# Two transformer blocks on one core: the last down product's second token tile in three pieces, and a last store of 256 columns

## The chip, the cores and the metric

One NeuronCore of a Trainium2 chip runs the whole program in one launch. The metric is the device time of that launch in microseconds. Three runs of the kernel before took 749.52, 749.52 and 749.61 us; their median is 749.52 us.

## The reference

The input is one sequence of 256 tokens by 1024 channels (float32). A first block (three mixers, then a gated feed-forward) and a second block (spatial gating, block-sparse attention, convolution, cross attention, then a feed-forward of 4096 hidden channels) follow each other. The change touches only the end of the second block, its last two lines:

```python
        h = rms_norm(x, pre_ffn_g[l])
        f = jnp.square(jax.nn.relu(h @ w_ff1[l])) @ w_ff2[l]
        x = x + rms_norm(f, post_ffn_g[l])
    return x
```

`rms_norm(f, g)` divides each token's 1024 values by the root of their mean square (plus 1e-6) and multiplies by `g`. So no element of the output can be formed before the last of the token's 1024 sums of `h @ w_ff2` is complete.

## The kernel before, in words

Tokens lie in two tiles of 128 (`t` = 0, 1), one token to a partition; `P` = 128, `T` = 256, `NB` = 512, `TT` = 2. Each float32 weight is split into a high part (ACT, a rounding copy) and a low part (DVE, L1318, raw minus high), and so is each activation; `mm3` (L2076 to L2080) makes one product from three matmuls: low activations by high weights, high by low, high by high. The program is written as one instruction stream for each engine (PE, ACT, DVE, POOL, and SP, which issues most DMAs), with semaphores between them. Each engine works through its stream in the written order.

The second feed-forward runs in 8 chunks of 512 hidden channels. The down product adds over all chunks into four banks of PSUM, each 128 partitions by 512 float32: banks 4 and 5 hold the left and right half (columns 0 to 511, 512 to 1023) of token tile 0, banks 6 and 7 those of token tile 1. The last chunk is done by `last_down` (L2155): token tile 0 first, both halves together (24 matmuls of 512 columns: 4 k-tiles, 2 halves, 3 matmuls), then token tile 1's left half (12 matmuls into bank 6), then its right half (12 into bank 7). PE raises `tile0_used` after tile 0 and after the left half, and `w_used` after each weight group of the right half.

What follows is `post_acc`, written once for ACT (L1093) and once for DVE (L1801). For each token tile, in the order tile 0, tile 1:

- ACT squares each half from its bank and adds up each row into `sums` (the Square with `accum_out`, traced as an ACTIVATE and an ACTIVATION_READ_ACCUMULATOR), and raises `post_sum`.
- DVE multiplies each half by the feed-forward's scale `inv` and the gain `row_g` into `xn` (L1809, "the gain" below), and raises `zg`; between the halves it adds 1e-6 to the first half's sum (L1812).
- ACT takes the root of both sums together (Sqrt with the other sum as bias) and raises `post_sd`.
- DVE takes the reciprocal (L1815), then adds `xn` times it to `x`, half by half (L1819, "the final sums"), and raises `x_ready` for each.

The same semaphore `zg` counts the gains of an earlier `post_norm` too: 8 of them before `post_acc` begins. SP waits for each `x_ready` in turn and issues four stores of 128 tokens by 512 columns (256 KB, rows of 2 KB; L562), then waits until all four have landed (L563), and that ends the program. ACT and DVE each finish tile 0's part of `post_acc` before they take up tile 1's, in the written order.

Of the kernel before, what the change touches and what calls it, by code (L numbers as in the profile page):

```python
# [14 lines left out]
P = 128  # L15
T = 256
# [242 lines left out]
def two_blocks(nc, w, out):  # L259
# [3 lines left out]
    with ctx:  # L263
        def sb(name, shape, dt=F32):
            return ctx.enter_context(nc.sbuf_tensor(name, shape, dt))
# [32 lines left out]
        inv = sb("inv", [P, 2 * TT])  # L298
        half_rstd = sb("half_rstd", [P, TT])
        sums = sb("sums", [P, TT, 2])  # L300
        var = sb("var", [P, 32])
        rstd = sb("rstd", [P, 32])
        tiny = sb("tiny", [P, 40])
# [187 lines left out]
        NORM_GAIN = ["norm_mix_g", "norm_ffn_g", "pre_mix_g_2", "mem_g_2", "pre_x_g_2", "pre_ffn_g_2"]  # L491
        X_READY_END = 4 + 4 + 2 + 5 * TT
        FINAL, POST = 6, 7
        SQRT_2_PI = math.sqrt(2 / math.pi)
        block = ctx.enter_context(nc.Block())

# [29 lines left out]
        def _(sp):  # L526
# [29 lines left out]
                                 src[row:row + n * P, c:c + cw].rearrange("(k p) n -> p k n", p=P))\  # L556
                      .then_inc(raw_in[g % RAW], 16)

            for t in range(TT):
                for c in range(2):  # L560
                    sp.wait_ge(sem.x_ready, X_READY_END - 2 * TT + 1 + 2 * t + c)
                    sp.dma_start(out[t * P:(t + 1) * P, c * NB:(c + 1) * NB], x[:, t, c * NB:(c + 1) * NB])\  # L562
                      .then_inc(sem.stored, 16)  # L563
            sp.wait_ge(sem.stored, 32 * TT)

        @block.gpsimd
        def _(pool):
# [150 lines left out]
        def _(act):  # L718
# [3 lines left out]
            def f(dst, src, func, **k):  # L722
                return act.activation(dst, src, func, **k)  # L723
# [369 lines left out]
            def post_acc():  # L1093
                for t in range(TT):
                    act.wait_ge(sem.ffn_scale, t + 1)
                    for c in range(2):
                        if c == 0:
                            act.wait_ge(sem.tile0_used, me.seen("tile0_used"))
                        elif t == 1:
                            act.wait_ge(sem.w_used, me.used)  # L1100
                        f(post_junk[:, t, c * NB:(c + 1) * NB], bank[4 + 2 * t + c][:, :], ACT.Square,
                          scale=inv[:, TT + t:TT + t + 1], accum_out=sums[:, t, c:c + 1]).then_inc(sem.post_sum, 1)
                    k = 2 * (POST + 2) + t
                    act.wait_ge(sem.post_sum, 8 + 2 * t + 2)
                    act.wait_ge(sem.left_sum, t + 1)
                    f(rstd[:, k:k + 1], sums[:, t, 1:2], ACT.Sqrt, bias=var[:, k:k + 1]).then_inc(sem.post_sd, 1)

            def x_exp(i):

# [192 lines left out]
        def _(dve):  # L1302
# [498 lines left out]
            def post_acc():  # L1801
                for t in range(TT):
                    k = 2 * (POST + 2) + t
                    for c in range(2):
                        dve.wait_ge(sem.post_sum, me.seen("post_sum"))
                        if c == 0 and t == 0:
                            dve.wait_ge(sem.row_in, me.seen("row_in", 16))
                        cut = slice(c * NB, (c + 1) * NB)
                        stt(xn[:, t, cut], bank[4 + 2 * t + c][:, :], inv[:, t:t + 1], row_g[:, cut], MUL, MUL)\  # L1809
                            .then_inc(sem.zg, 1)  # L1810
                        if c == 0:
                            ts(var[:, k:k + 1], sums[:, t, 0:1], EPS, None, ADD).then_inc(sem.left_sum, 1)  # L1812
                    dve.wait_ge(sem.zg, me.seen("zg", 2))
                    dve.wait_ge(sem.post_sd, t + 1)
                    dve.reciprocal(rstd[:, k:k + 1], rstd[:, k:k + 1]).then_inc(sem.dve_step, 1)  # L1815
                    dve.wait_ge(sem.dve_step, me.step())
                    for c in range(2):
                        cut = slice(c * NB, (c + 1) * NB)
                        stt(x[:, t, cut], xn[:, t, cut], rstd[:, k:k + 1], x[:, t, cut], MUL, ADD)\  # L1819
                            .then_inc(sem.x_ready, 1)  # L1820

            def kv_low(c, pair):
# [247 lines left out]
        def _(pe):  # L2070
# [85 lines left out]
            def last_down(c):  # L2156

                parts = chunks[("down2", c)]
                for t in range(TT):
                    for ns in ((0, 1),) if t == 0 else ((0,), (1,)):  # L2160
                        for g, kts in parts:
                            pe.wait_ge(low_sem(g), before(g))
                            wh, wl = part(high, g), part(low, g)
                            for j, kt in enumerate(kts):
                                in_h, in_l = (half[:, kt, t * P:(t + 1) * P] for half in hidden_of(c, False))
                                for n in ns:
                                    cut = slice(n * NB, (n + 1) * NB)
                                    ins = mm3(bank[4 + 2 * t + n][:, :], in_h, in_l, wh[:, j, cut], wl[:, j, cut],
                                              False, kt == 3)
                            if t == 1 and ns == (1,):  # L2170
                                ins.then_inc(sem.w_used, 1)
                        if t == 0 or ns == (0,):
                            ins.then_inc(sem.tile0_used, 1)

            def branch_products(i, mid=None):
# [509 lines left out]
```

## Time and profile before

| what | value |
|---|---|
| median of three runs | 749.52 us (749.52 to 749.61) |
| the profiled execution's own time | 749.77 us |
| its span (first to last event on the core) | 748.0 us |
| PE busy, share of the span | 740.5 us, 99% |
| DVE busy | 523.8 us, 70% |
| ACT busy | 402.5 us, 54% |
| POOL busy | 49.7 us, 7% |
| granted TensorE clock, mean | 1.0 of full speed |

The profile comes from one execution, whose own time is 0.25 us above the median and 1.77 us above its span. Times in the views are counted from the span's start, in microseconds, durations of groups in nanoseconds. PE is the matmul stream, PEld the loading of weights into it, DVE the vector engine, ACT the scalar engine, SPq the queue of SP's DMA issues. A matmul's end is modelled, its start is recorded. "idle" in a row is the engine's time without work just before, and what ended it.

### The profile page before, as it was taken

To read this page: it belongs to the slowest core of one execution; us is meant where nothing else is said; L and a number is where in the kernel's file an instruction comes from. 1 tells how busy PE (TensorE), PEld (TensorE's weight loads), DVE (VectorE), ACT (ScalarE), POOL (GpSimd) and SP (SyncE) were. 2 spreads that over 40 slices of the span, in tenths; PEclk is the share of its full clock that TensorE was granted. 3 is DMA by queue.
4 is the path that set the end of the run, shared out by engine and by line. 5 is a ranking of instruction groups with operands and counts; after the bars stand their busy time and mean duration, and the time that the engine had idled before them with its cause. 6 is when DMAs were issued, how large, how long until landed. Compare 5 with 4: busy or idle time off the path is not lost.

```text
span 748.0 us, 10384 instructions
## 1 busy us (share of the span) xinstructions
PE 740.5 (99%) x4280; PEld 648.8 (87%) x4280; DVE 523.8 (70%) x612; ACT 402.5 (54%) x509; POOL 49.7 (7%) x71
## 2 busy tenths in 40 slices
PE   9999999999999999999999999999999999999996
PEld 9988888889988888888899898789988988888885
DVE  6788946885766666656779998785758655556564
ACT  6678378544545545444653685673647443454442
POOL 0200002120000000000230200030003000000000
PEclk9999999999999999999999999999999999999999
DMA  9866365555565556666466536365065466555431
GB/s 337 280 224 225 137 237 210 171 171 168 176 219 169 170 171 204 215 203 209 154 218 205 165 117 225 116 235 165 21 212 166 162 221 225 172 199 188 162 123 57
DMA packets 74239, 138.42 MB, mean 185 GB/s; under 512 B 3916, under 2 KB 28368, under 8 KB 74064
## 3 DMA queue, kind: packets, MB, share of 16 engines
q1 hardware_dynamic: 72336, 132.69, 52.9%
q10 hardware_dynamic: 1856, 5.06, 1.9%
q8 instruction: 34, 0.56, 0.3%
q14 instruction: 13, 0.11, 0.0%
HBM read 136.69 MB, written 1.05 MB: 184 GB/s over the span
## 4 chain that ended last, share of the span: by engine, by line
PE 97%; DVE 2%; issue 0%; ACT 0%; DVEq 0%; ACTq 0%
PE wide L2074 70%; PE bank L2074 25%; PE bank L2198 2%; DVE low L1318 0%; DVE arena L1581 0%; ACT arena L723 0%; DVE act_hl L1415 0%; DVE xn L1809 0%; DVE x L1819 0%; DVE arena L1641 0%; DVE arena L1637 0%; DVE hid_l L1646 0%; DVE arena L1643 0%; DVE arena L1627 0%; DVEq L263 0%
## 5 line engine op out<-in xcount | busy, mean ns | idle before, releaser
L1318 DVE TENSOR_TENSOR low<-raw,high 128x2048 fp32r<-128x2048 f32 (+1 forms) x118 | 267.0, 2279 | 106.2 <-ACT high L723 101.5
L723 ACT ACTIVATE high<-raw 128x2048 fp32r<-128x2048 f32 (+3 forms) x134 | 234.7, 1770 | 122.8 <-PE wide L2074 95.9
L2074 PE MATMUL wide<-act_hl,high 128*128 128x256 f32 (+1 forms) x1184 | 241.3, 327 | 0.0
L2074 PEld LDWEIGHTS wide<-act_hl,high 128*128 128x128 f32 x1184 | 198.9, 191 | 18.3 <-issue 0.2
L2074 PE MATMUL wide<-high,act_hl 128*128 128x512 f32 x528 | 170.1, 394 | 0.5 <-DVE arena L1581 0.2
L2074 PE MATMUL wide<-act_hl,low 128*128 128x256 f32 x832 | 161.2, 284 | 0.0
L2074 PEld LDWEIGHTS wide<-act_hl,low 128*128 128x128 f32 x832 | 128.6, 192 | 2.8 <-DVE low L1366 0.2
L2074 PEld LDWEIGHTS wide<-high,act_hl 128*128 128x128 f32 x528 | 99.1, 188 | 23.3 <-issue 1.7
L2074 PE MATMUL wide<-low,act_hl 128*128 128x512 f32 x264 | 103.0, 390 | 0.0
L2074 PE MATMUL bank<-high,hid_l 128*128 128x512 f32 x216 | 84.4, 391 | 0.3 <-DVE hid_l L1646 0.3
L2074 PE MATMUL bank<-low,hid_h 128*128 128x512 f32 x216 | 84.2, 390 | 0.0
L2074 PE MATMUL bank<-high,hid_h 128*128 128x512 f32 x216 | 84.0, 389 | 0.0
L723 ACT ACTIVATE arena<-wide 128x512 f32<-128x512 f32 x53 | 29.5, 596 | 86.3 <-PE wide L2074 86.3
L2074 PEld LDWEIGHTS wide<-low,act_hl 128*128 128x128 f32 x264 | 49.7, 188 | 9.3
L2074 PEld LDWEIGHTS bank<-high,hid_l 128*128 128x128 f32 x216 | 40.6, 188 | 8.6 <-DVE hid_l L1646 0.7
L2074 PEld LDWEIGHTS bank<-high,hid_h 128*128 128x128 f32 x216 | 40.6, 188 | 8.6
L2074 PEld LDWEIGHTS bank<-low,hid_h 128*128 128x128 f32 x216 | 40.6, 188 | 7.8
L1627 DVE TENSOR_TENSOR arena<-wide,arena 128x512 f32<-128x512 f32 x30 | 20.7, 689 | 28.7 <-ACT arena L723 28.5
L1442 DVE SCALAR_TENSOR_TENSOR arena<-arena,vec 128x256 f32<-128x256 f32 x78 | 38.3, 536 | 0.9
L723 ACT ACTIVATE hid_h<-arena 128x512 fp32r<-128x512 f32 x27 | 16.8, 635 | 29.0 <-DVE arena L1643 16.9
L723 ACT ACTIVATE arena<-arena 128x512 f32<-128x512 f32 (+5 forms) x31 | 19.5, 651 | 21.4 <-DVE arena L1637 14.5
L588 POOL TENSOR_SCALAR var<-sums 128x1 f32<-128x1 f32 x8 | 6.0, 748 | 316.1 <-ACT xn L723 208.5
(215 smaller groups left out, 681.1 us busy)
## 6 DMA issues: line engine op xcount, KB each, us to landing
raw<-in_w_ff_dram SPq DMA_DIRECT2D x32, 1024.0 KB, 5.3
raw<-in_w_in_dram SPq DMA_DIRECT2D x27, 1024.0 KB, 5.3
raw<-in_w_ffn_in_dram SPq DMA_DIRECT2D x44, 512.0 KB, 4.9
raw<-in_w_ffn_out_dram SPq DMA_DIRECT2D x11, 1024.0 KB, 6.5
raw<-in_w_xkv_dram SPq DMA_DIRECT2D x8, 1024.0 KB, 5.0
raw<-in_w_o_dram SPq DMA_DIRECT2D x4, 1024.0 KB, 5.1
raw<-in_w_out_dram SPq DMA_DIRECT2D x4, 1024.0 KB, 5.0
raw<-in_w_xq_dram SPq DMA_DIRECT2D x4, 1024.0 KB, 5.2
```

Of the source, the lines that this page charges most:

```text
L588: pool.tensor_scalar(v, sums[:, t, 0:1], sums[:, t, 1:2], EPS, ALU.add, ALU.add)\
L723: return act.activation(dst, src, func, **k)
L1318: tt(part(low, g), part(raw, g), f32(part(high, g)), SUB).then_inc(sem.low_by_dve, 1)
L1442: ins = stt(tile_of(dst, c), window, weight(j, c), tile_of(dst, c), MUL, ADD)
L1627: tt(in2(h_low[b]), wide_of(b, 0), in2(h_low[b]), ADD).then_inc(sem.hid_sum, 1)
L2074: return pe.matmul(dst, lhs, rhs, start=start, stop=stop, skip_group_check=loose)
L2198: return pe.transpose(dst, src, ident[0:n, 0:n])
```

## The change

`last_down` does token tile 1 in three pieces, named by `LAST_SPANS`: columns 512 to 767 (the third quarter, in the first half of bank 7), columns 0 to 511 (the left half, bank 6), and columns 768 to 1023 (the fourth quarter, in the second half of bank 7). Before the third piece PE waits until `zg` is 11 (`FIRST_OUT`): 8 earlier gains, 2 of tile 0, and tile 1's first one, of the third quarter. `post_acc` handles tile 1 in the same three pieces on both engines, with a third sum `third_sum`; DVE adds the first two sums and 1e-6 after the second gain. The final sums of tile 1 are of 256, 512 and 256 columns. The stores of tile 1 are three: the third quarter's is issued from ACT's queue, those of the left half and the fourth quarter from SP's. `stored` is waited for to 80 instead of 64 (five stores).

```diff
+        third_sum = sb("third_sum", [P, 1])
...
+        LAST_SPANS = (NB, T), (0, NB), (NB + T, T)
+        FIRST_OUT = 2 * 2 * TT + 2 + 1
+        last_sums = (sums[:, 0, 0:1], sums[:, 0, 1:2]), (sums[:, 1, 0:1], sums[:, 1, 1:2], third_sum[:, :])
...
-            for t in range(TT):
-                for c in range(2):
-                    sp.wait_ge(sem.x_ready, X_READY_END - 2 * TT + 1 + 2 * t + c)
-                    sp.dma_start(out[t * P:(t + 1) * P, c * NB:(c + 1) * NB], x[:, t, c * NB:(c + 1) * NB])\
-                      .then_inc(sem.stored, 16)
-            sp.wait_ge(sem.stored, 32 * TT)
+            for i, (t, a, size) in enumerate(((0, 0, NB), (0, NB, NB), (1, 0, NB), (1, NB + T, T))):
+                sp.wait_ge(sem.x_ready, X_READY_END - 2 * TT + (1, 2, 4, 5)[i])
+                sp.dma_start(out[t * P:(t + 1) * P, a:a + size], x[:, t, a:a + size]).then_inc(sem.stored, 16)
+            sp.wait_ge(sem.stored, 80)
...
             def post_acc():
                 for t in range(TT):
                     act.wait_ge(sem.ffn_scale, t + 1)
-                    for c in range(2):
-                        if c == 0:
+                    for i, (a, size) in enumerate(LAST_SPANS if t else ((0, NB), (NB, NB))):
+                        if i < 2 and i <= t:
                             act.wait_ge(sem.tile0_used, me.seen("tile0_used"))
                         elif t == 1:
                             act.wait_ge(sem.w_used, me.used)
-                        f(post_junk[:, t, c * NB:(c + 1) * NB], bank[4 + 2 * t + c][:, :], ACT.Square,
-                          scale=inv[:, TT + t:TT + t + 1], accum_out=sums[:, t, c:c + 1]).then_inc(sem.post_sum, 1)
+                        f(post_junk[:, t, a:a + size], bank[4 + 2 * t + a // NB][:, a % NB:a % NB + size], ACT.Square,
+                          scale=inv[:, TT + t:TT + t + 1], accum_out=last_sums[t][i]).then_inc(sem.post_sum, 1)
                     k = 2 * (POST + 2) + t
-                    act.wait_ge(sem.post_sum, 8 + 2 * t + 2)
+                    act.wait_ge(sem.post_sum, 8 + (2, 5)[t])
                     act.wait_ge(sem.left_sum, t + 1)
-                    f(rstd[:, k:k + 1], sums[:, t, 1:2], ACT.Sqrt, bias=var[:, k:k + 1]).then_inc(sem.post_sd, 1)
+                    f(rstd[:, k:k + 1], last_sums[t][-1], ACT.Sqrt, bias=var[:, k:k + 1]).then_inc(sem.post_sd, 1)
+                act.wait_ge(sem.x_ready, X_READY_END - 1)
+                act.dma_start(out[P:2 * P, NB:NB + T], x[:, 1, NB:NB + T]).then_inc(sem.stored, 16)
...
-                    for c in range(2):
+                    spans = LAST_SPANS if t else ((0, NB), (NB, NB))
+                    for i, (a, size) in enumerate(spans):
                         dve.wait_ge(sem.post_sum, me.seen("post_sum"))
...
+                        stt(xn[:, t, a:a + size], bank[4 + 2 * t + a // NB][:, a % NB:a % NB + size], inv[:, t:t + 1],
+                            row_g[:, a:a + size], MUL, MUL).then_inc(sem.zg, 1)
+                        if t == 0 and i == 0:
                             ts(var[:, k:k + 1], sums[:, t, 0:1], EPS, None, ADD).then_inc(sem.left_sum, 1)
+                        elif t == 1 and i == 1:
+                            ts(var[:, k:k + 1], sums[:, t, 0:1], sums[:, t, 1:2], EPS, ADD, ADD).then_inc(sem.left_sum, 1)
...
-                    for ns in ((0, 1),) if t == 0 else ((0,), (1,)):
+                    for piece in range(1 if t == 0 else 3):
+                        spans = LAST_SPANS[piece:piece + 1] if t else ((0, NB), (NB, NB))
+                        if piece == 2:
+                            pe.wait_ge(sem.zg, FIRST_OUT)
                         for g, kts in parts:
...
-                            if t == 1 and ns == (1,):
+                            if t == 1 and piece == 2:
                                 ins.then_inc(sem.w_used, 1)
-                        if t == 0 or ns == (0,):
+                        if t == 0 or piece < 2:
                             ins.then_inc(sem.tile0_used, 1)
```

PE's stream at the border between the last two pieces of token tile 1. Before, from the left half (bank 6) to the right half (bank 7):

```order
L2074 MATMUL bank6<-high0,hid_l1 128x512
L2074 MATMUL bank6<-low0,hid_h1 128x512
L2074 MATMUL bank6<-high0,hid_h1 128x512
L2074 MATMUL bank7<-high2,hid_l1 128x512 [waits low_by_dve]
L2074 MATMUL bank7<-low2,hid_h1 128x512
L2074 MATMUL bank7<-high2,hid_h1 128x512
```

and in the change, from the left half to the fourth quarter:

```order
L2079 MATMUL bank6<-high0,hid_l1 128x512
L2079 MATMUL bank6<-low0,hid_h1 128x512
L2079 MATMUL bank6<-high0,hid_h1 128x512
L2079 MATMUL bank7<-high2,hid_l1 128x256 [waits low_by_dve,zg]
L2079 MATMUL bank7<-low2,hid_h1 128x256
L2079 MATMUL bank7<-high2,hid_h1 128x256
```

The last piece has 12 matmuls of 256 columns instead of 12 of 512, and its first one waits for `zg`; 12 more of 256 columns into bank 7 now stand ahead of the left half's.

DVE's stream from tile 0's final sums on. Before:

```order
L1819 SCALAR_TENSOR_TENSOR x<-xn,rstd,x 128x512 [waits dve_step]
L1819 SCALAR_TENSOR_TENSOR x<-xn,rstd,x 128x512
L1809 SCALAR_TENSOR_TENSOR xn<-bank6,inv,row_g 128x512 [waits post_sum]
L1812 TENSOR_SCALAR var<-sums 128x1
L1809 SCALAR_TENSOR_TENSOR xn<-bank7,inv,row_g 128x512 [waits post_sum]
L1815 RECIPROCAL rstd<-rstd 128x1 [waits post_sd,zg]
L1819 SCALAR_TENSOR_TENSOR x<-xn,rstd,x 128x512 [waits dve_step]
L1819 SCALAR_TENSOR_TENSOR x<-xn,rstd,x 128x512
```

and in the change:

```order
L1824 SCALAR_TENSOR_TENSOR x<-xn,rstd,x 128x512 [waits dve_step]
L1824 SCALAR_TENSOR_TENSOR x<-xn,rstd,x 128x512
L1813 SCALAR_TENSOR_TENSOR xn<-bank7,inv,row_g 128x256 [waits post_sum]
L1813 SCALAR_TENSOR_TENSOR xn<-bank6,inv,row_g 128x512 [waits post_sum]
L1818 TENSOR_SCALAR var<-sums 128x1
L1813 SCALAR_TENSOR_TENSOR xn<-bank7,inv,row_g 128x256 [waits post_sum]
L1821 RECIPROCAL rstd<-rstd 128x1 [waits post_sd,zg]
L1824 SCALAR_TENSOR_TENSOR x<-xn,rstd,x 128x256 [waits dve_step]
L1824 SCALAR_TENSOR_TENSOR x<-xn,rstd,x 128x512
L1824 SCALAR_TENSOR_TENSOR x<-xn,rstd,x 128x256
```

The third quarter's gain, whose `zg` PE waits for, stands right behind tile 0's two final sums, and the small addition of the sums has moved behind the second gain.

## Rows read from the trace of the kernel before

**Rows 1.** the page, part 4: the chain that ended last, shares of the span

```profile
PE 97%; DVE 2%; issue 0%; ACT 0%; DVEq 0%; ACTq 0%
```

**Rows 2.** timeline (start us, us, engine, line, operation, tiles): ACT and DVE to the end

```profile
740.18 0.67 ACT L723 ACTIVATE arena<-bank,inv 128x512 f32<-128x512 f32 x1
...
740.57 1.42 DVE L1819 SCALAR_TENSOR_TENSOR x<-xn,rstd,x 128x512 f32<-128x512 f32 x2
...
741.90 0.74 DVE L1809 SCALAR_TENSOR_TENSOR xn<-bank,inv,row_g 128x512 f32<-128x512 f32 x1
...
742.36 0.69 ACT L723 ACTIVATE arena<-bank,inv 128x512 f32<-128x512 f32 x1 [1.42 <-PE bank L2074]
...
742.94 0.19 ACT L723 ACTIVATION_READ_ACCUMULATOR arena<-bank,inv 128x1 f32 x1
...
743.17 0.75 DVE L1809 SCALAR_TENSOR_TENSOR xn<-bank,inv,row_g 128x512 f32<-128x512 f32 x1 [0.47 <-ACT arena L723]
743.96 0.16 DVE L1815 RECIPROCAL rstd<-rstd 128x1 f32<-128x1 f32 x1
744.15 1.42 DVE L1819 SCALAR_TENSOR_TENSOR x<-xn,rstd,x 128x512 f32<-128x512 f32 x2
```

**Rows 3.** SP's queue in the timeline: the last store's issue

```profile
745.59 0.33 SPq L562 DMA_DIRECT2D out_dram<-x  x1
```

**Rows 4.** the output stores' line: time to landing

```profile
DMA to landing us min/median/max: 2.0/2.0/2.1
```

**Rows 5.** timeline of PE: token tile 1's first and last matmul

```profile
736.72 0.39 PE L2074 MATMUL bank<-high,hid_l 128*128 128x512 f32 x1
...
741.93 0.39 PE L2074 MATMUL bank<-high,hid_h 128*128 128x512 f32 x1
```

**Rows 6.** timeline of PE: sixteen matmuls of 256 columns in a row

```profile
718.46 2.08 PE L2074 MATMUL wide<-act_hl,low 128*128 128x256 f32 x16
```

**Rows 7.** instructions grouped by line and shape, DVE: xcount, busy us, mean ns, idle

```profile
L1442 DVE SCALAR_TENSOR_TENSOR arena<-arena,vec 128x256 f32<-128x256 f32 x78 | 38.3, 536 | 0.9
...
L1383 DVE SCALAR_TENSOR_TENSOR act_hl<-bank,vec,act_hl 128x256 fp32r<-128x256 f32 x24 | 9.8, 477 | 2.9 <-ACT act_hl L723 2.9
...
L1809 DVE SCALAR_TENSOR_TENSOR xn<-bank,inv,row_g 128x512 f32<-128x512 f32 x4 | 3.0, 747 | 7.3 <-ACT arena L723 7.3
...
L1512 DVE SCALAR_TENSOR_TENSOR arena<-arena 128x256 f32<-128x256 f32 x2 | 0.8, 425 | 0.1
```

**Rows 8.** timeline: PE held by DVE and started again, an earlier down product

```profile
357.61 0.69 DVE L1646 TENSOR_TENSOR hid_l<-arena,hid_h 128x512 fp32r<-128x512 f32 x1 [0.70 <-ACT hid_h L723]
...
358.35 0.50 PE L2074 MATMUL bank<-high,hid_l 128*128 128x512 f32 x1 [0.26 <-DVE hid_l L1646]
...
358.69 0.40 PE L2074 MATMUL bank<-low,hid_h 128*128 128x512 f32 x1
```

**Rows 9.** instructions grouped by line and shape, ACT

```profile
L723 ACT ACTIVATE arena<-wide,half_rstd 128x512 f32<-128x512 f32 x12 | 7.6, 685 | 11.0 <-PE wide L2074 11.0
...
L723 ACT ACTIVATE arena<-bank,neg_max,rstd 128x256 f32<-128x256 f32 x8 | 4.5, 560 | 8.1 <-DVE neg_max L1856 8.0
...
L723 ACT ACTIVATE arena<-wide,half_rstd 128x256 f32<-128x256 f32 x2 | 0.9, 450 | 0.0
```

**Rows 10.** timeline of DVE: eight operations of 256 columns in a row

```profile
133.31 3.25 DVE L1383 SCALAR_TENSOR_TENSOR hid_l<-xn,vec,hid_h 128x256 fp32r<-128x256 f32 x8
```

**Rows 11.** stretches: us, PE, PEld, DVE, ACT, POOL busy (x), PEclk, DMA share, GB/s

```profile
745.00:746.00 1.00, 0.00 (x0) 0.00 (x0) 0.57 (x1) 0.00 (x0) 0.00 (x0) 1.00 0.22 84
746.00:747.00 1.00, 0.00 (x0) 0.00 (x0) 0.00 (x0) 0.00 (x0) 0.00 (x0) 1.00 1.04 385
...
747.40:748.00 0.60, 0.00 (x0) 0.00 (x0) 0.00 (x0) 0.00 (x0) 0.00 (x0) 0.53 0.00 0
```

**Rows 12.** DMA issues of loads: xcount, KB each, median us to landing

```profile
raw<-in_w_ff_dram SPq DMA_DIRECT2D x32, 1024.0 KB, 5.3
...
raw<-in_w_ffn_in_dram SPq DMA_DIRECT2D x44, 512.0 KB, 4.9
```

More of the change, by code:

```diff
@@ L1803, in post_acc @@
                     k = 2 * (POST + 2) + t
-                    for c in range(2):
+                    spans = LAST_SPANS if t else ((0, NB), (NB, NB))
+                    for i, (a, size) in enumerate(spans):
                         dve.wait_ge(sem.post_sum, me.seen("post_sum"))
-                        if c == 0 and t == 0:
+                        if i == 0 and t == 0:
                             dve.wait_ge(sem.row_in, me.seen("row_in", 16))
[L1808 to L1811, printed above, removed]
+                        stt(xn[:, t, a:a + size], bank[4 + 2 * t + a // NB][:, a % NB:a % NB + size], inv[:, t:t + 1],
+                            row_g[:, a:a + size], MUL, MUL).then_inc(sem.zg, 1)
+                        if t == 0 and i == 0:
                             ts(var[:, k:k + 1], sums[:, t, 0:1], EPS, None, ADD).then_inc(sem.left_sum, 1)
-                    dve.wait_ge(sem.zg, me.seen("zg", 2))
+                        elif t == 1 and i == 1:
+                            ts(var[:, k:k + 1], sums[:, t, 0:1], sums[:, t, 1:2], EPS, ADD, ADD).then_inc(sem.left_sum, 1)
+                    dve.wait_ge(sem.zg, me.seen("zg", len(spans)))
                     dve.wait_ge(sem.post_sd, t + 1)
@@ L1816, in post_acc @@
                     dve.wait_ge(sem.dve_step, me.step())
-                    for c in range(2):
-                        cut = slice(c * NB, (c + 1) * NB)
-                        stt(x[:, t, cut], xn[:, t, cut], rstd[:, k:k + 1], x[:, t, cut], MUL, ADD)\
+                    for a, size in spans:
+                        stt(x[:, t, a:a + size], xn[:, t, a:a + size], rstd[:, k:k + 1], x[:, t, a:a + size], MUL, ADD)\
                             .then_inc(sem.x_ready, 1)
@@ L2165, in last_down @@
                                 in_h, in_l = (half[:, kt, t * P:(t + 1) * P] for half in hidden_of(c, False))
[L2166 to L2169, printed above, removed]
-                            if t == 1 and ns == (1,):
+                                for a, size in spans:
+                                    cut = slice(a, a + size)
+                                    ins = mm3(bank[4 + 2 * t + a // NB][:, a % NB:a % NB + size], in_h, in_l,
+                                              wh[:, j, cut], wl[:, j, cut], False, kt == 3)
+                            if t == 1 and piece == 2:
                                 ins.then_inc(sem.w_used, 1)
-                        if t == 0 or ns == (0,):
+                        if t == 0 or piece < 2:
                             ins.then_inc(sem.tile0_used, 1)
```

## The prediction

> **What bounds the kernel now.** I read the page's chain first: 97% of the span is PE's work [rows 1], so until the last down product nothing but PE's own pace counts, and the change leaves all of that alone. What is left is the end, and for it I read the timeline of the last engines [rows 2] and SP's queue [rows 3]. PE's last matmul starts at 741.93 and ends, as modelled, at 741.93 + 0.39 = 742.32 [rows 5]. Then one thing follows another: the Square of the right half (742.36), its accumulator read (742.94), the right half's gain on DVE (743.17), the reciprocal (743.96), two final sums (744.15 to 745.57) [rows 2], the last store's issue at 745.59 [rows 3] and its landing 2.0 us later [rows 4], at 747.59. The span ends 0.4 us after that. The reader is to see two things: the tail from PE's end to the landing is 5.27 us, in which halving the last piece can save something; and DVE is not idle before it. Tile 0's final sums run from 740.57 to 741.99, and only then, at 741.90 (the rows overlap by 0.08), does DVE take the left half's gain, although ACT had squared that half from 740.18 on [rows 2]. DVE is late with tile 0 when tile 1 comes.
>
> **PE's pieces.** Twelve matmuls of 512 columns become 24 of 256. 512 columns come every (741.93 - 736.72) / 23 = 0.227 us [rows 5]; sixteen of 256 take 2.08 us, the last one 0.28, so one every 0.12 us [rows 6]. Without any wait, the third quarter would run from 736.72 to 738.16, the left half to 740.88, and the fourth quarter's last matmul would start at 742.20 and end at 742.48: 0.16 later than before.
>
> **The new wait.** The fourth quarter's first matmul waits for the third quarter's gain. ACT can have squared that quarter by about 740.8: it starts at 740.18 as it now starts the left half [rows 2], and the piece is smaller. But on DVE the gain stands behind tile 0's two final sums, which nothing in the change moves. It takes the place that the left half's gain has now, 741.90 [rows 2]. A gain of 256 columns isn't in the trace. The nearest row is DVE's operation of the same kind, from a bank with a per-token scalar, 477 ns (bounds: 425 without the scalar, 536 for the slowest of 256 columns; 512 columns take 747) [rows 7]. So `zg` reaches 11 at 741.90 + 0.48 = 742.38. An earlier down product shows what a restart costs: DVE's operation ended at 357.61 + 0.69 = 358.30, PE started at 358.35, and the second matmul came 0.34 after the first instead of 0.23 [rows 8]. So PE starts at 742.43, its twelfth matmul at 742.43 + 0.11 + 11 x 0.12 = 743.86, and it ends at 744.14. PE stands for 742.43 - 740.88 = 1.55 us, and ends **1.82 us later** than before. Behind the waiting instruction on PE is only this piece, and ACT's last Square waits for it. The left half's gain meanwhile runs on DVE from 742.30 to 743.05, and the addition of the sums behind it, both under PE's last piece: nothing. If that cover went, they would add 0.75 + 0.14.
>
> **The tail behind it.** The Square of 256 columns: a pair of rows gives 685 ns for 512 columns and 450 for 256 of the same operation, so 0.24 less (bound: an accumulating one of 256 took 560, only 0.12 less) [rows 9]. The gain: 0.75 to 0.48, 0.27 less; the Sqrt beside it (0.29) is still shorter. The reciprocal stays. The final sums: two of 512 columns took 1.42. Now there are three. Eight operations of 256 columns took 3.25 us, the last one 0.48, so one every 0.40 [rows 10]; 512 ones come 1.42 - 0.75 = 0.67 apart. 0.40 + 0.67 + 0.48 = 1.55, 0.13 more. Sum on DVE: +1.82 - 0.24 - 0.27 + 0.13 = +1.44, so its last sum ends at 747.01, and its first begins at 747.01 - 1.55 = 745.46.
>
> A rule speaks against the change here. The Trainium skill, page "VectorE: DVE Perf Modes", section on the TRN2 errata, says that operations pay a fixed part each and should be of 512 elements or more. Its estimate for float32, (N + 151) / 0.96 ns, gives 424 ns for 256 columns and 691 for 512; by it the gain that PE waits for is 0.05 shorter, the last gain saves 0.27 as above, and three sums cost 0.16 us more than two, so the sum would be +1.42. The trace agrees with the slope (270 ns for 256 columns, 747 less 477) if not with the level.
>
> **The stores.** Before, the two stores of tile 1 moved 524 KB: 84 KB up to 746, 385 KB in the next microsecond, the rest after it [rows 11]. At 385 GB/s they were done at 747.14, 0.45 before the landing, and a 256 KB store takes 0.68, so its data begins 2.0 - 0.45 - 0.68 = 0.87 after the issue. Now the third quarter's store is issued by ACT near 745.97 and is through by 747.2. The left half's sum ends at 745.46 + 0.40 + 0.75 = 746.61, its store is issued at 746.63, its data begins at 747.50. The fourth quarter's is issued at 747.03, so its data would begin at 747.90, but the left half's occupy the engines until 748.18. 393 KB from 747.50 take 1.02: 748.52, landing at 748.97, **+1.38**. If landing were 2.0 whatever the size, it would be 749.03, +1.44. Whether rows of 1 KB move as fast as rows of 2 KB: weight loads of two times 512 KB (1 KB rows) land after 4.9 us, of 1024 KB (2 KB rows) after 5.3 [rows 12]; the second half is issued some 0.4 later, so yes. Two queues in place of one, and the fifth store's semaphore, I cost at nothing: the third quarter's store has over 1 us of cover.
>
> **Sum:** +1.4 us. Bounds: no restart cost, and gains at 425: -0.11 - 0.05 - 0.05 - 0.05, so +1.1. Gains at 536, the Square at 560, the last store at the full 0.68: +0.06 for each of three operations, +0.11, +0.34, so +2.0. The profiled execution would take 749.77 + 1.4 = 751.2; it stands 0.25 above the median, so against the median of 749.52 I forecast **750.9 us**. That is 0.19%, and 0.2% (1.5 us) is about what a measurement of this kernel can tell from no change: the forecast lies just inside it.
>
> **Rivals.**
> 1. *The last store costs a whole one* (slower, beyond 0.2%). If 128 rows of 1 KB occupy the DMA engines as long as 128 rows of 2 KB, the last landing moves by 0.34: +1.7, 751.2 us. It decides from 0.1 us above my sum on. For it: the store waits behind the left half's. Against it: rows 12. I count with it the case that small operations stand near their upper bounds. 27%.
> 2. *The clock falls in the gap.* At 1.2 instead of 2.4 GHz the twelve matmuls would take 1.3 us more: +2.7, 752.2 us. Against it: after PE's end the granted clock was still 1.00 at 746 to 747, over 4 us later, and only then 0.53 [rows 11]; the gap is 1.55 us. 3%.
> 3. *PE isn't held.* If `zg` passes before 740.9, because the count or DVE's order is another than the text says, PE ends at 742.48: +0.16 - 0.24 - 0.27 + 0.13 - 0.06 = -0.3 us, 749.2 us. That is what the change would give if DVE were free in time. Against it: the 8 earlier gains and tile 0's two leave 11 to tile 1's first, and DVE's order is fixed. 4%, of which 1% for more than 0.2% faster.
>
> **The numbers.** The forecast has 66%, 11 of them above +1.5. Slower by over 0.2%: 11 + 27 + 3 = 41%; faster 1%; within 0.2%, the rest: 58%. The range takes the bounds +1.1 to +2.0 and goes a little beyond them, to 750.4 and 751.6; it leaves out rivals 2 and 3 and the far tails.
>
> **What would show it.** PE idle from about 740.9 to 742.4, released by DVE's gain, twelve matmuls of 256 columns behind it at clock 1.00, PE's end near 744.1; Square about 0.45, gains about 0.48, three final sums in 1.55; last store issued near 747.0, span near 749.4. The argument is wrong if PE shows no gap, if the gap ends at another time than DVE's first small gain, or if the last landing comes over 2.1 us after its issue.

## The result

| | before | the change |
|---|---|---|
| median, 14 runs each | 749.56 us (749.06 to 750.07) | 751.02 us (750.58 to 751.36) |
| ratio to before, 95% interval | | 1.0019 [1.0012, 1.0026] |
| span of the profiled execution | 748.0 us | 749.3 us |
| granted TensorE clock, mean | 1.0 | 0.999 |

The kernel became slower by 1.46 us; the forecast was 1.4 us, 750.9, in a range of 750.4 to 751.6. By the 0.2% that the text had set, it lies just within "no change", yet the interval excludes 1: with 14 runs a side it is 0.07% wide to each side, finer than that bound. Of the runs below, one of twelve of the kernel "third quarter early" (4046.16 us) and one of eleven of that kernel with halves and the early table (2616.61 us) took several times as long, at a mean granted clock of 1.0 and for a reason that no trace shows; the medians include them (without them 749.40 in place of 749.44 and 749.18 in place of 749.19), the ratios do not.

The page of the kernel after: its first line, and the busy times.

```profile
span 749.3 us, 10414 instructions
...
PE 740.7 (99%) x4292; PEld 649.5 (87%) x4292; DVE 523.9 (70%) x614; ACT 402.8 (54%) x511; POOL 49.7 (7%) x71
```

PE has twelve more matmuls and 0.2 us more work; nothing there explains 1.5 us. The end of the timeline does (start us, us, engine, line, operation, tiles, count, in brackets the idle time before it and what ended it). The rows answer to [rows 2] and [rows 5].

```profile
740.32 0.19 ACT L725 ACTIVATION_READ_ACCUMULATOR arena<-bank,inv 128x1 f32 x1
740.36 1.41 DVE L1824 SCALAR_TENSOR_TENSOR x<-xn,rstd,x 128x512 f32<-128x512 f32 x2
740.46 0.39 PE L2079 MATMUL bank<-high,hid_h 128*128 128x512 f32 x1
...
741.69 1.14 DVE L1813 SCALAR_TENSOR_TENSOR xn<-bank,inv,row_g 128x256 f32<-128x256 f32 x2
...
742.22 0.39 PE L2079 MATMUL bank<-high,hid_l 128*128 128x256 f32 x1 [1.37 <-DVE xn L1813]
...
742.44 0.28 PE L2079 MATMUL bank<-low,hid_h 128*128 128x256 f32 x1
...
743.64 0.28 PE L2079 MATMUL bank<-high,hid_h 128*128 128x256 f32 x1
743.95 0.47 ACT L725 ACTIVATE arena<-bank,inv 128x256 f32<-128x256 f32 x1 [2.29 <-PE bank L2079]
744.33 0.19 ACT L725 ACTIVATION_READ_ACCUMULATOR arena<-bank,inv 128x1 f32 x1
...
744.55 0.48 DVE L1813 SCALAR_TENSOR_TENSOR xn<-bank,inv,row_g 128x256 f32<-128x256 f32 x1 [1.61 <-ACT arena L725]
745.07 0.16 DVE L1821 RECIPROCAL rstd<-rstd 128x1 f32<-128x1 f32 x1
745.27 1.54 DVE L1824 SCALAR_TENSOR_TENSOR x<-xn,rstd,x 128x256 f32<-128x256 f32 x3
```

In this execution everything up to token tile 1 came 0.22 us earlier than in that of before: tile 1's first matmul starts at 736.50, before at 736.72 [rows 5]. Below, times are therefore compared from that first matmul on, called T0. The reader is to see: ACT has read the third quarter's sum by 740.51 (740.32 + 0.19), but DVE is busy until 741.77 with tile 0's two final sums and takes the third quarter's gain at 741.69, the first of the two operations in that row. The left half's last matmul starts at 740.46, so PE was ready for the fourth quarter at 740.69; its next matmul starts at 742.22. That is T0 + 5.72, where the forecast had T0 + 5.71. The list of waits names the releaser (who waited, for whom; us in all, times, longest):

```profile
PE bank L2079 <- DVE xn L1813: 1.4, 1, 1.4
```

The 1.37 us are counted from the modelled end of the matmul before; from the moment at which PE could have gone on it is 1.53.

The granted clock stays whole over the gap and behind it (columns as in [rows 11]):

```profile
741.00:742.00 1.00, 0.00 (x0) 0.00 (x0) 1.00 (x3) 0.66 (x2) 0.00 (x0) 1.00 0.02 8
742.00:743.00 1.00, 0.78 (x6) 0.79 (x7) 0.94 (x3) 0.00 (x0) 0.00 (x0) 1.00 1.00 373
743.00:744.00 1.00, 0.92 (x8) 0.71 (x6) 0.00 (x0) 0.05 (x1) 0.00 (x0) 1.00 0.38 143
```

The last store's issue on SP's queue, the third quarter's on ACT's, and the landings (issues: count, KB each, median us to landing):

```profile
746.84 0.48 SPq L565 DMA_DIRECT2D out_dram<-x  x1
```

```profile
745.79 0.35 ACTq L1110 DMA_DIRECT2D out_dram<-x  x1
```

```profile
out_dram<-x SPq DMA_DIRECT2D x3, 256.0 KB, 2.1
out_dram<-x ACTq DMA_DIRECT2D x1, 128.0 KB, 1.8
out_dram<-x SPq DMA_DIRECT2D x1, 128.0 KB, 2.1
```

The last store of 128 KB is issued at 746.84 and lands 2.1 us later, no sooner than a store of 256 KB [rows 4]; alone, the third quarter's lands after 1.8.

### The profile page after: what moved, and what is told of

Read it like the earlier page. It is cut to its first block, busy times and chain, and to the rows that moved or that the text cites. A ratio compares the mean times of both kernels' runs of the same rounds, so it can differ in the third digit from the quotient of the medians.

```text
span 749.3 us, 10414 instructions
## 1 busy us (share of the span) xinstructions
PE 740.7 (99%) x4292; PEld 649.5 (87%) x4292; DVE 523.9 (70%) x614; ACT 402.8 (54%) x511; POOL 49.7 (7%) x71
## 3 DMA queue, kind: packets, MB, share of 16 engines
q10 hardware_dynamic: 2000, 5.19, 1.9%
## 4 chain that ended last, share of the span: by engine, by line
PE 93%; DVE 2%; DMA 2%; issue 1%; ACT 1%; SPq 0%; POOL 0%; DVEq 0%; ACTq 0%; POOLq 0%
PE wide L2079 67%; PE bank L2079 24%; PE bank L2206 2%; DMA x<-in_x_dram 1%; DMA raw<-in_w_in_dram 1%; DVE low L1322 0%; DVE x L1824 0%; ACT arena L725 0%; DVE arena L1585 0%; DVE xn L1813 0%; DVE act_hl L1419 0%; DVE low L1370 0%; POOL rstd L596 0%; ACT act_hl L725 0%; DVE hid_l L1650 0%
## 5 line engine op out<-in xcount | busy, mean ns | idle before, releaser
L2079 PE MATMUL bank<-high,hid_l 128*128 128x512 f32 (+1 forms) x220 | 85.2, 387 | 1.6 <-DVE xn L1813 1.4
L2079 PE MATMUL bank<-low,hid_h 128*128 128x512 f32 (+1 forms) x220 | 85.0, 386 | 0.0
L2079 PE MATMUL bank<-high,hid_h 128*128 128x512 f32 (+1 forms) x220 | 84.7, 385 | 0.0
```

Of the source, the lines that this page charges most:

```text
L2079: return pe.matmul(dst, lhs, rhs, start=start, stop=stop, skip_group_check=loose)
```

## The experiments

All medians below are of timed runs beside runs of the kernel before on the same chip. There are three such series, in which the kernel before took 749.53, 749.60 and 749.62 us (749.56 beside the change), so times of different series compare only to about 0.1 us. In a trace, "ready" is the start of the left half's last matmul plus 0.23 us, and PE's gap is the fourth quarter's first matmul less ready. The texts that were written ahead of the runs partly count it from the modelled end of the matmul before, which makes it 0.16 us shorter (1.37 for 1.53, 2.17 for 2.33).

### The third quarter early

```diff
 ACT:
+                    if t == 0:
+                        act.wait_ge(sem.ffn_scale, 2)
+                        act.wait_ge(sem.tile0_used, me.seen("tile0_used"))
+                        square(1, 0, *LAST_SPANS[0])
                     k = 2 * (POST + 2) + t
 DVE:
+                    if t == 0:
+                        gain(1, *LAST_SPANS[0])
                     dve.wait_ge(sem.zg, ...)
                     dve.wait_ge(sem.post_sd, t + 1)
                     dve.reciprocal(...)
```

(Shortened: `square` and `gain` are the change's own operations, put into helpers, and tile 1's own loops leave out the third quarter, which is already done.)

> Edit: on ACT the Square of the third quarter, and on DVE its gain, go ahead of token tile 0's root and reciprocal; all else is as in the change. Theory A (the change pays for PE's wait behind DVE's two final sums of tile 0, one for one): the gain ends near 739.5, before PE is ready for the fourth quarter (740.7 in the change's trace), so PE has no gap, neither the 1.53 us of standing nor the 0.11 us of restart; 751.0 - 1.6 = 749.4 us, span near 747.7. Theory B (the 1.5 us lie in the smaller operations and the fifth store): they are all still there, so the time stays within 0.4 us of 751.0.

Measured: 749.44 us, before 749.53, ratio 0.9998 [0.9989, 1.0007]. The timeline of DVE and PE:

```profile
738.01 1.13 DVE L1817 SCALAR_TENSOR_TENSOR xn<-bank,inv,row_g 128x512 f32<-128x512 f32 x2
...
740.30 1.42 DVE L1841 SCALAR_TENSOR_TENSOR x<-xn,rstd,x 128x512 f32<-128x512 f32 x2
740.31 0.28 PE L2096 MATMUL bank<-high,hid_l 128*128 128x256 f32 x1
...
741.63 0.28 PE L2096 MATMUL bank<-high,hid_h 128*128 128x256 f32 x1
```

The gain is the second of the two operations at 738.01 and over at 739.14, in time in which DVE used to wait for the root. PE's fourth quarter starts at 740.31 without a gap and ends at 741.91. The 1.6 us are gone, while the small operations and the fifth store are all still there. Theory B falls.

### The third quarter between tile 0's final sums

```diff
                     for i, (a, size) in enumerate(spans):
+                        if t == 0 and i == 1:
+                            gain(1, *LAST_SPANS[0])
                         stt(x[:, t, a:a + size], ...)
```

> Edit: on DVE alone, the gain of the third quarter goes between tile 0's two final sums instead of behind both. Theory A: zg reaches 11 one final sum (0.67 us) earlier, PE restarts near 741.55 on the change's clock instead of 742.22, and the time falls by 0.67 to 750.3 us. Theory B: no effect, 751.0 us.

Measured: 750.47 us, ratio 1.0011 [1.0003, 1.002]. One operation moved by one place on one engine:

```profile
740.94 0.48 DVE L1808 SCALAR_TENSOR_TENSOR xn<-bank,inv,row_g 128x256 f32<-128x256 f32 x1
...
741.33 0.74 DVE L1832 SCALAR_TENSOR_TENSOR x<-xn,rstd,x 128x512 f32<-128x512 f32 x1
...
741.47 0.39 PE L2087 MATMUL bank<-high,hid_l 128*128 128x256 f32 x1 [0.79 <-DVE xn L1808]
```

PE starts 0.05 us behind the end of the gain (741.42). Its gap is 0.95 us (the left half's last matmul starts at 740.29), 0.58 less than the change's, and the time 0.55 less.

### The root's table early

```diff
             def post_acc():
+                f(loaded[:, :], ones[:, 0:1], ACT.Sqrt)
                 for t in range(TT):
                     act.wait_ge(sem.ffn_scale, t + 1)
```

> Edit: one Sqrt of a single column on ACT ahead of the last part, while ACT is idle, so that the table for the root is loaded there and not between tile 0's Squares and its root (1.28 us). DVE's order stays as in the change. Theory A, one step further back (DVE is late with tile 0 because of the table load): tile 0's root is taken near 738.45, its final sums run from 739.3 to 740.7, the third quarter's gain ends near 741.1, PE's gap shrinks from 1.53 to about 0.5, the time falls by 1.0 to 750.0 us. Theory B, or a table load that is not what delays DVE: 751.0 us.

Measured: 749.87 us, ratio 1.0006 [0.9997, 1.0014]. In the change, ACT loads the table between tile 0's Squares and its root:

```profile
738.47 1.28 ACT L725 ACT_TABLE_LOAD   x1 [0.25 <-DVE var L1816]
```

and here that load is gone from this place:

```profile
738.20 0.29 ACT L725 ACTIVATE rstd<-sums,var 128x1 f32<-128x1 f32 x1 [0.27 <-DVE var L1817]
...
739.00 1.42 DVE L1825 SCALAR_TENSOR_TENSOR x<-xn,rstd,x 128x512 f32<-128x512 f32 x2
...
740.33 0.48 DVE L1814 SCALAR_TENSOR_TENSOR xn<-bank,inv,row_g 128x256 f32<-128x256 f32 x1
...
740.87 0.19 PEld L2080 LDWEIGHTS bank<-high,hid_l 128*128 128x128 f32 x1 [0.72 <-DVE xn L1814]
```

Tile 0's root is taken at 738.20, and DVE's final sums begin at 739.00, 2.77 us after T0 (736.23) instead of 3.86. The gain stands where it stood in the order, and PE's gap is 0.46 us (the left half's last matmul starts at 740.18). So the reason that DVE is late with tile 0 is shown too: the table load of 1.28 us between tile 0's Squares and its root.

### The early third quarter with halves at the end

```diff
-                    for a, size in spans:
+                    for a, size in ((0, NB), (NB, NB)):
                         stt(x[:, t, a:a + size], ...)
 SP: four stores of 512 columns as before; ACT's store goes; stored is waited for to 64
```

> Edit: as in the first of these kernels (third quarter early on ACT and DVE), but tile 1's final sums are two of 512 columns and its stores two of 256 KB from SP, as before the change. Theory A with the terms of the sum: two sums take 0.13 us less than three, and the last store of 256 KB, with no store to wait behind, lands 2.0 us after its issue; so 0.0 to 0.1 us faster than the first kernel, 749.3 us. Theory C (the last store of 256 columns is worth having): the first kernel is faster than this one by 0.2 to 0.3 us, the half transfer of 0.34 less the 0.13.

Measured: 749.08 us, before 749.53, ratio 0.9993 [0.9985, 1.0002]; faster than the first of these kernels by 0.36 us at the medians and by 0.21 in T0 to the span's end (10.96 against 11.17). Two final sums take

```profile
743.47 1.41 DVE L1839 SCALAR_TENSOR_TENSOR x<-xn,rstd,x 128x512 f32<-128x512 f32 x2
```

against 1.54 for three. Theory C falls: a last store of 256 columns brings nothing here. In the two traces three pieces of sums and five stores cost 0.21 us, more than the expected 0.0 to 0.1: 0.13 up to DVE's last sum (T0 + 8.67 against T0 + 8.54) and 0.08 behind it. How much more than that the 0.36 of the medians holds stays open, since the kernel "the order of the last sums" below has three sums and five stores too and came out 0.39 under its own kernel before, almost as far as this one (0.45).

### Both, and the early table in the kernel before

```diff
 the kernel "early third quarter with halves", and on ACT
             def post_acc():
+                f(loaded[:, :], ones[:, 0:1], ACT.Sqrt)
```

> Edit: the kernel with the third quarter early and tile 1's final sums and stores in halves, and in addition the root's table loaded early (one Sqrt of a single column before the last part). Theory A: PE no longer waits for DVE in either, so an earlier tile 0 has little left to give; DVE's left gain and the addition of the sums (742.29 to 742.71 in the first kernel's trace) end just at the last gain's start, and going early frees at most 0.05 us: 749.0 to 749.1 us, level with the kernel without it (749.08). Rival: DVE's lateness with tile 0 costs the end on its own, apart from PE's wait; then it is faster by 0.3 or more.

Measured: 749.19 us, before 749.60, ratio 0.9991 [0.9982, 1.0001]; T0 to the span's end 10.96 us, the same as without the early table.

```diff
 the kernel before, and on ACT
             def post_acc():
+                f(loaded[:, :], ones[:, 0:1], ACT.Sqrt)
```

> Edit: the kernel before, with the root's table loaded early and nothing else. Theory A: in the kernel before, DVE's lateness with tile 0 is hidden, since its left gain (to 742.6) is over before the right half's sum is read (743.13), so nothing changes: 749.5 us. Rival, as for the kernel above: the time falls by 0.3 or more, and part of what the early table gained in the change was not PE's wait.

Measured: 749.55 us, before 749.60, ratio 1.0002 [0.9992, 1.0011]; T0 to the span's end 11.30 us (747.8 less 736.50), against 11.28 in the kernel before. Together these two say that DVE's lateness with tile 0 costs nothing by itself: it is hidden in the kernel before and in the kernel with the third quarter early. Only the change's wait made it visible. So the 1.15 us that the early table brought to the change are put down to PE's wait, which was 1.07 us shorter.

### The third quarter's gain one place later

```diff
-        FIRST_OUT = 2 * 2 * TT + 2 + 1
+        FIRST_OUT = 2 * 2 * TT + 2 + 2
...
-                    for i, (a, size) in enumerate(spans):
+                    order = [(0, *spans[0]), (1, *spans[1])] if t == 0 else [(1, *spans[1]), (0, *spans[0]), (2, *spans[2])]
+                    for i, a, size in order:
```

(Shortened: DVE's waits for the sums follow the new order; ahead of the left half's gain it waits for two sums.)

> Edit: in the change, DVE does the left half's gain first and the third quarter's behind it, so that PE waits for the twelfth gain in place of the eleventh. Nothing else moves. Theory A: zg arrives one operation of 512 columns (0.67 us) later, PE's gap grows from 1.53 to 2.2 us and the time by 0.67 to 751.7 us. Theory B (the gap is mostly cover for something else): less than 0.3 us more.

Measured: 752.52 us (751.43 to 752.87, 5 runs), ratio 1.0036 [1.0023, 1.0049]. Neither theory had this: one run of five took 751.4, the other four 752.4 to 752.9, 0.8 us more than the wait accounts for.

```profile
742.26 0.47 DVE L1814 SCALAR_TENSOR_TENSOR xn<-bank,inv,row_g 128x256 f32<-128x256 f32 x1
742.78 0.29 PEld L2080 LDWEIGHTS bank<-high,hid_l 128*128 128x128 f32 x1 [2.59 <-DVE xn L1814]
...
743.16 0.42 PE L2080 MATMUL bank<-low,hid_h 128*128 128x256 f32 x1
...
745.30 0.41 PE L2080 MATMUL bank<-high,hid_h 128*128 128x256 f32 x1
```

The gap is 2.32 us, as meant (742.78 less 740.46). But the matmuls of 256 columns behind it come 0.21 us apart instead of 0.12. The stretches tell why (PEclk is the third figure from the end):

```profile
740.60:742.60 2.00, 0.02 (x1) 0.00 (x0) 2.00 (x5) 0.78 (x2) 0.00 (x0) 1.00 0.43 158
742.60:742.90 0.30, 0.12 (x1) 0.12 (x1) 0.13 (x1) 0.00 (x0) 0.00 (x0) 0.83 1.04 396
742.90:743.40 0.50, 0.50 (x3) 0.50 (x4) 0.00 (x0) 0.00 (x0) 0.00 (x0) 0.50 0.48 180
743.40:745.70 2.30, 2.30 (x11) 2.02 (x10) 0.00 (x0) 0.00 (x0) 0.00 (x0) 0.50 0.00 0
```

The granted clock is 1.00 until 742.6, that is over the 2 us in which PE stands, and 0.50 from 742.9 on. The mean of 0.83 in between puts the fall to 1.2 GHz near 742.8, in this trace just as PE restarts, and all of the last piece runs under it. The last matmul ends at T0 + 9.43 (745.30 + 0.41 less 736.28).

### The gap filled

```diff
 the kernel "one place later", and on PE
                         if piece == 2:
+                            for _ in range(8):
+                                mm(bank[0][:, 0:P], ones[:, :], ones[:, :])
                             pe.wait_ge(sem.zg, FIRST_OUT)
```

> Edit: the kernel with the third quarter's gain behind the left half's (PE's gap 2.17 us; 752.5 us, and the granted clock fell to 0.5 for the fourth quarter), and in PE's gap, ahead of the wait, eight matmuls of ones by ones into a bank that nothing reads any more. They compute nothing that is used. If the 0.8 us beyond the expected 751.7 were the clock's and the idle gap brought its fall on, the granted clock stays 1.0 with PE at work, the last twelve matmuls come 0.12 us apart again and the time is 751.7 us in all runs. If something else slows them (a bank, a weight load after a long wait), they stay 0.21 apart and the time stays 752.5.

Measured: 751.88 us (751.45 to 752.00, 7 runs), ratio 1.0028 [1.0017, 1.004]. None of them took the longer time, 752.3 to 752.9, that most runs of the unfilled kernels took.

The trace records the eight calls as sixteen matmuls:

```profile
740.64 1.95 PE L2080 MATMUL wide<-ones 128*128 128x128 f32 x16
...
742.97 0.39 PE L2080 MATMUL bank<-high,hid_l 128*128 128x256 f32 x1 [0.38 <-DVE xn L1814]
...
744.38 0.28 PE L2080 MATMUL bank<-high,hid_h 128*128 128x256 f32 x1
```

```profile
743.00:744.00 1.00, 1.00 (x8) 1.00 (x9) 0.00 (x0) 0.00 (x0) 0.00 (x0) 1.00 0.32 121
```

DVE still releases PE 2.33 us after it was ready (742.97 less 740.64), and the matmuls behind it are 0.12 apart again. The unfilled gap brought the clock's fall; the last piece's bank, weight loads and order are the same in both kernels. PE ends at T0 + 8.20 (744.38 + 0.28 less 736.46), 1.23 us before the unfilled kernel's T0 + 9.43; rival 2 had priced the lower clock at 1.3. What is left over the kernel without a gap is 751.88 - 749.44 = 2.44 us, and 2.33 + 0.11 for the restart is 2.44. (These two were measured in different series; each less its own kernel before, the difference is 2.26 + 0.09 = 2.35.)

### The later gain with the early table

```diff
 the kernel "one place later", and on ACT
             def post_acc():
+                f(loaded[:, :], ones[:, 0:1], ACT.Sqrt)
```

> Edit: the same kernel (third quarter's gain behind the left half's) with the root's table loaded early and no filling. DVE is through with tile 0 early, but now waits for the left half's sum (read at 741.4), so the third quarter's gain ends near 742.5 and PE's gap is about 1.9 us, between the change's 1.37 to 1.53 and the 2.17 where the clock fell in four runs of five. At clock 1.0: the change plus 0.35, 751.4 us. Where the clock falls: 752.2 us. If the fall needs a certain length of idle time near 2 us, both kinds of runs appear or none is slow; if only gaps beyond 2.1 do it, all are near 751.4.

Measured: 752.67 us, ratio 1.0037 [1.0024, 1.0049], one run at 751.50, four at 752.3 to 752.9, on the same chip as the filled kernel. The edit missed its aim, a gap in between: DVE was free early, but ACT read the left half's sum no sooner than before, and the gap came out as

```profile
742.31 0.47 DVE L1815 SCALAR_TENSOR_TENSOR xn<-bank,inv,row_g 128x256 f32<-128x256 f32 x1
742.84 0.29 PEld L2081 LDWEIGHTS bank<-high,hid_l 128*128 128x128 f32 x1 [2.59 <-DVE xn L1815]
```

742.84 less 740.51, 2.33 us, the same as without the table. So it is a repetition, and it repeats: one run of five at the shorter time. One thing is new:

```profile
742.00:743.00 1.00, 0.16 (x1) 0.16 (x1) 0.78 (x3) 0.00 (x0) 0.00 (x0) 0.84 0.14 49
743.00:744.00 1.00, 1.00 (x5) 1.00 (x6) 0.00 (x0) 0.00 (x0) 0.00 (x0) 0.50 0.00 0
```

A mean of 0.84 over 742 to 743, with 0.50 behind it, puts the fall at 742.68, 0.16 us before the restart at 742.84: here the clock fell while PE still stood. What the record holds of the fall is these two traces. For the other runs it is read from their times: of the eight longer ones six, the two traced among them, have a mean granted clock of 0.995 to 0.997, and two (752.52 and 752.43 us) have 1.0 and 0.999, which shows nothing either way. Between 1.53 us (no longer time in 25 runs, 14 of the change and 11 of the change with halves) and 2.3 (the longer time in eight runs of ten) no gap was tried.

### The order of the last sums

```diff
 the kernel "third quarter early", and
-                    for a, size in spans:
+                    for a, size in (((0, NB), (NB, T), (NB + T, T)) if t else spans):
                         stt(x[:, t, a:a + size], ...)
```

> Edit: the kernel with the third quarter early, its final sums of tile 1 in the order left half, third quarter, fourth quarter, with the stores in that order too. Operations and bytes are the same. If the last store is late because it waits behind the left half's transfer (as the forecast's sum had it: 0.28 us of waiting), the wait shrinks to 0.22 and the landing comes 0.06 earlier: 749.4 us, not to be told from 749.44 by the time, but the last store lands 2.0 us or less after its issue instead of 2.1. If a small store as such needs that long, 2.1 us stays.

Measured: 749.21 us, ratio 0.9993 [0.9984, 1.0002], T0 to the span's end 11.22 us against 11.17. Both small stores now land 2.1 us after their issue, the last one too. The expected 0.06 can't be seen; the median is 0.23 below that of the kernel with the other order (749.44, in another series), which the two traces do not show. Whether the small store is slow by itself or by its neighbours stays open: alone, with nothing in front of it, it took 1.8.

### The change with halves at the end

```diff
 the change, with the edits on sums and stores of the kernel "early third quarter with halves"
```

> Edit: the change with its wait, but tile 1's final sums two of 512 columns and its stores two of 256 KB, as before. If the parts of the sum add up, what these parts saved without the wait (749.44 to 749.08, 0.36 us) they save with it too: 750.7 us, span 0.2 to 0.35 shorter than the change's. If the last small store is of use behind a late PE, it is 751.0 or more.

Measured: 750.71 us, before 749.62, ratio 1.0016 [1.0007, 1.0025]; T0 to the span's end 12.66 us against the change's 12.80. The time is the expected 750.7; the span shrank by 0.14, a little less than expected. So the parts add up, to about 0.1 us.

### The ladder

| kernel | gap, us | gap + 0.11 restart | time, less 749.44 | T0 to span's end, less 11.17 |
|---|---|---|---|---|
| third quarter early | 0 | 0 | 749.44, 0 | 736.13 to 747.3, 0 |
| table early | 0.46 | 0.57 | 749.87, 0.43 | 736.23 to 748.0, 0.60 |
| third between the sums | 0.95 | 1.06 | 750.47, 1.03 | 736.34 to 748.6, 1.09 |
| the change | 1.53 | 1.64 | 751.02, 1.58 | 736.50 to 749.3, 1.63 |
| later and filled | 2.33 | 2.44 | 751.88, 2.44 | 736.46 to 750.1, 2.47 |

Five kernels with the same operations in `post_acc`, which differ in their places, a table load and the filling, lie on one line: each microsecond in which PE waits for that gain is a microsecond of the program, plus 0.11 once. The spans keep to it within 0.03 us and the medians within 0.14; with each median less its own kernel before and without the run of 4046 us, the steps are 0.47, 1.07, 1.59 and 2.39.

## Why the prediction was right

**What bounds the end.** PE, then one chain behind it. Right; the ladder shows it.

**PE's pieces.** Said: 0.12 us a matmul, the fourth quarter's ready point at T0 + 4.16 (740.88 less 736.72). Measured T0 + 4.19.

**The new wait.** Said: the gain takes the place of the left half's, T0 + 5.18, and PE restarts at T0 + 5.71, ending at T0 + 7.42. Measured: 5.19, 5.72 and 743.64 + 0.28, T0 + 7.42. The duration of the gain (0.48), which no row of before had, and the restart (the second matmul 0.22 behind the first instead of 0.12) came out as the nearest rows had them. This step was read off the order of DVE's stream against the start of one row; the mean busy share of DVE (70%) would have said that there was room.

**The tail.** Said: Square 0.45, gain 0.48, three sums 1.55, DVE's end at T0 + 10.29. Measured 0.47, 0.48, 1.54, and T0 + 10.31. The rule of "VectorE: DVE Perf Modes" in the Trainium skill (section on the TRN2 errata), that operations should be of 512 elements or more, is borne out in this trace for the final sums, where three cost 0.13 more than two on the path. It is no guide to the last gain: there the smaller piece shortens what stands behind PE by 0.27 (0.75 to 0.48), and the other pieces are done under PE's work.

**The stores.** This is the term that was mis-sized. Said: the last landing 1.94 us after its issue (748.97 less 747.03), because 128 KB move in half the time; the span would end at T0 + 12.65. Measured: 2.1 us, and T0 + 12.80. The step was that small stores save the time of half their bytes [rows 12]; that was argued from loads of 512 KB, and the landings of 128 KB stores did not bear it out. From the last store's issue to the span's end it is 2.46 us (746.84 to 749.3), where the sum had 2.34, so 0.12 to 0.16 of the difference is the store's. It is rival 1, at a third to a half of its price of 0.34. It makes the profiled spans differ by 1.52 from T0 on (12.80 against 748.0 - 736.72 = 11.28 before), where the sum had 1.38; the medians of the runs lie between, at 1.46.

**Rival 2, the clock.** Given 3%, and in the change it did not occur: all 14 runs lie within 0.8 us. But the reason given against it was not a good one. It said that after PE's end the clock had stayed whole for over 4 us [rows 11], and so a gap of 1.55 was far from it. In the kernels with a gap of 2.3 us it fell 2.2 and 2.0 us after the modelled end of PE's last matmul, and the longer time came in eight runs of ten. At the ends of the traces, too, the distance is not a fixed one. In the change's it fell 3.4 us after PE's end (near 747.3, by a mean of 0.66 over 747 to 748, after 743.92), and in that of the kernel with the root's table early 2.8 us after it (near 745.3, after 742.56):

```profile
745.00:746.00 1.00, 0.00 (x0) 0.00 (x0) 0.46 (x2) 0.00 (x0) 0.00 (x0) 0.67 0.44 152
```

against 5.1 in the kernel before (near 747.4, after 742.32). So the idle time ahead of a fall differs from trace to trace, here between 2.0 and 5.1 us, and a single trace in which it held does not show that a gap of half that length is safe. The change's gap was 0.8 us shorter than the one that lost the clock, not 2.5.

**Rival 3, PE not held.** Priced at 749.2, 0.3 us under before. The kernel that has it (third quarter early) took 749.44, 0.1 under. At the profiled spans the sum had -0.28 and the trace gives 11.17 against 11.28, -0.11; the difference is about the size of the stores' term again.

**What the change was worth without its wait.** A last piece of 256 columns instead of 512 shortens the tail: with the third quarter early and halves at the end, T0 to the span's end is 10.96 us against 11.28 before, 0.32 less, and at the medians 0.45 less, with the interval [0.9985, 1.0002] just reaching 1. The sister kernel with the early table has 0.9991 [0.9982, 1.0001]. The kernel with the left half's sum first has 0.9993 [0.9984, 1.0002]. These are the fastest versions seen; none is clear of the measurement's noise by itself.

Not tried: the fourth quarter without any wait on the third quarter's gain. PE would write a bank that DVE may be reading. The Trainium skill, "PSUM — Partial Sum Buffer", section on bank collisions, says that two engines must not use one bank of the same partitions at the same time, whatever the columns; no run here shows that, and the wait was moved in every kernel, never left out.

## What to carry to other kernels

When the last piece of a product is cut smaller so that its consumers have less to do, look at what the new wait asks of a consumer engine: not whether that engine has idle time, but which instructions stand ahead of the released one in its stream, and when the last of them ends. A consumer's lateness that is hidden today can become the producer's stall tomorrow; moving the one operation into the consumer's idle time (here the 1.1 us in which DVE waited for tile 0's root) cured it at no cost that these runs show (749.44 us against 749.53 before). And a stall on PE can have a second price beyond its length, the clock: with 2.3 us it came in most runs here, with 1.53 in none.

## What the runs showed of the hardware that was not expected

- The clock fell with a much shorter idle stretch than the profile of before suggested. With 2.3 us between PE's ready point and its restart, it fell to 0.50 near 742.8, at the restart (742.78), in one trace and at 742.68, before the restart (742.84), in the other, and matmuls of 256 columns came 0.21 us apart instead of 0.12. Over the two kernels with that gap unfilled, eight runs of ten showed the longer time and two did not. With 1.53 us, no run of 25 did.
- How long PE was idle before the clock fell was not the same from trace to trace: 2.0 and 2.2 us in those two, 2.8, 3.4 and 5.1 at the ends of the three other traces read above.
- Sixteen small matmuls in the gap (1.95 us) kept the clock at 1.00 in the trace and the longer time away in seven runs of seven.
- A store of 128 rows of 1 KB landed 1.8 us after its issue when alone and 2.1 us close behind another one; 128 rows of 2 KB took 2.0 to 2.1 us. Halving a store saved 0.2 us at most. SP's issue of the last small store took 0.48 us where [rows 3] have 0.33.
